# A decoder trunk on one core: one input tile taken in as two parts, three embedding products and two norms placed elsewhere

## The reference, cut to what matters

```python
def rmsnorm(x, g):  return x * lax.rsqrt(jnp.mean(x * x, -1) + EPS) * g

for i in range(DEPTH):                                   # DEPTH = 2
    f = swiglu(rmsnorm(h, P['g_f1_pre'][i]), ...)        # first feed-forward, width 2816
    h = h + 0.5 * rmsnorm(f, P['g_f1_post'][i])
    mo = mixer(rmsnorm(h, P['g_mix_pre'][i]), ...)       # pooling, short convolution, GLU convolution + layer norm
    h = h + rmsnorm(mo, P['g_mix_post'][i])
    f = swiglu(rmsnorm(h, P['g_f2_pre'][i]), ...)        # second feed-forward
    h = h + 0.5 * rmsnorm(f, P['g_f2_post'][i])
    gate = jax.nn.sigmoid(rmsnorm(h, P['g_ple_pre'][i]) @ P['w_ple_gate'][i])
    h = h + rmsnorm((p[i] @ P['w_ple_proj'][i]) * gate, P['g_ple_post'][i])
return rmsnorm(h, P['g_final'])
```

## Time and profile before

| what | value |
|---|---|
| median of three runs | 1551.94 us |
| the profiled execution's own time | 1550.16 us |
| its span, first to last instruction | 1548.2 us |
| PE busy | 1531.0 us, 99%, 10408 matmuls |
| DVE / ACT / POOL busy | 67% / 46% / 42% |
| mean granted PE clock | 0.997 |
| bytes moved | 229.31 MB, 148 GB/s on average |

### The profile page before, as it was taken

How to read it: one execution, slowest core, us unless ns; L and a number is a source line. 1 busy time by engine, 2 the same in 40 slices (tenths; PEclk the granted TensorE clock), 3 DMA queues, 4 the chain that set the end, 5 groups by cost and what they waited for, 6 DMA issues and landing times.

```text
span 1548.2 us, 28024 instructions
## 1 busy us (share of the span) xinstructions
PE 1531.0 (99%) x10408; PEld 1521.9 (98%) x10408; DVE 1034.7 (67%) x1588; ACT 713.4 (46%) x1057; POOL 643.5 (42%) x680
## 2 busy tenths in 40 slices
PE   9999999999999999999999999999999999999997
PEld 9999999999999999999999999999999999999997
DVE  7655437999876755634885553389997866555356
ACT  6333435445456433433653333355455554334346
POOL 3755203499330655500047551035973307554001
PEclk9999999999999999999999999999999999999998
DMA  6545432444443544632334454334444335445412
GB/s 221 170 154 181 172 129 84 163 151 148 163 137 109 187 161 137 226 141 93 123 125 167 144 193 169 119 110 141 159 153 148 118 128 191 157 142 213 146 70 82
DMA packets 52921, 229.31 MB, mean 148 GB/s; under 512 B 3824, under 2 KB 3952, under 8 KB 48496
## 3 DMA queue, kind: packets, MB, share of 16 engines
q1 hardware_dynamic: 52272, 226.07, 42.6%
q10 hardware_dynamic: 576, 2.26, 0.4%
HBM read 225.27 MB, written 3.04 MB: 147 GB/s over the span
## 4 chain that ended last, share of the span: by engine, by line
PE 92%; DVE 3%; issue 2%; ACT 1%; DMA 1%; POOL 0%; SPq 0%; DVEq 0%; POOLq 0%; ACTq 0%
PE ps L449 29%; PE ps L451 29%; PE ps L450 29%; PE ps L487 1%; PE ps L491 1%; PE ps L488 1%; DVE h L1184 0%; DVE w_lo_sb L1139 0%; DVE ga L1179 0%; PE ps L553 0%; DMA raw<-in_w_f_up 0%; DMA h<-in_x 0%; DVE x_lo L1194 0%; DVE ssq L1153 0%; PE ps L562 0%
## 5 line engine op out<-in xcount | busy, mean ns | idle before, releaser
L1139 DVE TENSOR_TENSOR w_lo_sb<-raw,w_hi_sb 128x1024 fp32r<-128x1024 f32 (+1 forms) x388 | 552.4, 1424 | 229.2 <-ACT w_hi_sb L812 228.5
L449 PE MATMUL ps<-x_hi,w_hi_sb 128*128 128x320 f32 x2232 | 693.1, 311 | 1.2 <-DVE w_lo_sb L1139 1.2
L451 PE MATMUL ps<-x_hi,w_lo_sb 128*128 128x320 f32 x2232 | 689.6, 309 | 0.0
L450 PE MATMUL ps<-x_lo,w_hi_sb 128*128 128x320 f32 x2232 | 689.6, 309 | 0.0
L812 ACT ACTIVATE w_hi_sb<-raw 128x1024 fp32r<-128x1024 f32 (+1 forms) x388 | 428.9, 1110 | 558.2 <-PE ps L451 465.0
L449 PEld LDWEIGHTS ps<-x_hi,w_hi_sb 128*128 128x128 f32 x2232 | 418.9, 188 | 3.2 <-DVE w_lo_sb L1139 1.1
L450 PEld LDWEIGHTS ps<-x_lo,w_hi_sb 128*128 128x128 f32 x2232 | 419.0, 188 | 0.6
L451 PEld LDWEIGHTS ps<-x_hi,w_lo_sb 128*128 128x128 f32 x2232 | 418.9, 188 | 0.0
L450 PE MATMUL ps<-mid_lo,w_hi_sb 128*128 128x320 f32 x704 | 217.4, 309 | 0.0
L449 PE MATMUL ps<-mid_hi,w_hi_sb 128*128 128x320 f32 x704 | 217.4, 309 | 0.0
L451 PE MATMUL ps<-mid_hi,w_lo_sb 128*128 128x320 f32 x704 | 217.4, 309 | 0.0
(11 more groups left out here) (209 smaller groups left out, 1636.0 us busy)
## 6 DMA issues: line engine op xcount, KB each, us to landing
raw<-in_w_f_up SPq DMA_DIRECT2D x86, 1024.0 KB, 5.3
raw<-in_w_f_dn SPq DMA_DIRECT2D x32, 1408.0 KB, 6.0
raw<-in_w_gate SPq DMA_DIRECT2D x24, 1024.0 KB, 5.3
raw<-in_w_out SPq DMA_DIRECT2D x12, 1024.0 KB, 5.2
raw<-in_w_glu SPq DMA_DIRECT2D x8, 1024.0 KB, 5.2
raw<-in_w_short SPq DMA_DIRECT2D x8, 1024.0 KB, 5.2
raw<-in_w_wo SPq DMA_DIRECT2D x8, 1024.0 KB, 5.2
raw<-in_w_pg SPq DMA_DIRECT2D x8, 1024.0 KB, 5.3
```

The costliest lines, as they stand in the source:

```text
L449: pe.matmul(out, whi, rhs_hi, start=start, stop=False, skip_group_check=True)
L450: pe.matmul(out, whi, rhs_lo, start=False, stop=False, skip_group_check=True)
L451: return pe.matmul(out, wlo, rhs_hi, start=False, stop=stop, skip_group_check=True)
L1139: dve.tensor_tensor(w_lo_sb[:, j, 0:n], raw[:, j, 0:n], w_hi_sb[:, j, 0:n].bitcast(F32), ALU.subtract).then_inc(w_lo, 1)
```

## The change

Five things change, in both layers.

At b1 the first three halves of `glu` get x tile 0 as two parts: g times the old h (tile 0), and g times f (tile 0), f being the output of the feed-forward ahead of its norm. ACT and DVE split both parts into x tiles 0 and 7 during `f1_dn`. PE multiplies the first part into the halves' own banks and the second into three others; these 18 matmuls take the place of the twelve filling ones. The chase then runs over tiles 1 to 7 and makes tile 0 last, for the fourth half alone. ACT copies the three banks of the second part to `sg`, DVE copies `bc` there, POOL multiplies the one by the other, and when DVE moves those three halves it adds the part first and then multiplies by `rb`.

At b2 three of the eight embedding products, with the part of the weights they need loaded and split during `wo`, take the place of the twelve filling matmuls. At b3 five products are left. The layer norm `ln` goes the way of `pre1`, with one wide matmul and a reciprocal of 128x320. The sums of `pre3` go from the fourth half of the first `pg` pair to the third x tile of the second pair, and their `spread` from its second to its seventh.

```diff
-        proj_raw = gate[...][:, 0:PROJ]
+        EARLY = 3
+        PROJ = (DT - EARLY) * PT * P
+        early_raw = bg[...][:, 0:EARLY_W]
-        PROJ_BANKS = (4, 5, 6, 3, 2, 0, 1, 3)
+        PROJ_BANKS = (0, 1, 2, 4, 5, 6, 3, 2)
-        SPREAD = ("post1", "ln", "post2", "post3", "pre3", "post4")
-        WIDE = (None, "pre1", "pre2")
+        SPREAD = ("post1", "post2", "post3", "pre3", "post4")
+        WIDE = (None, "pre1", "ln", "pre2")
+        def tile_at(n, i):
+            return (i + 1) % DT if n == 0 else i
+        H_PART, F_PART = 0, DT - 1
+        PART_BANKS = (2, 0, 1)
+        part_sum = [sg[:, j, :] for j in range(3)]
+        rinv_row = sg[:, 3, :]
...
# PE
+                n = new_hi[0]
+                last = DT - 2 if n == 0 else DT - 1
...
                 for k in range(DT):
                     wait_hi(k)
+                    if k > last:
+                        pe.wait_ge(x_ready, xl + k + 1)
+                        break
...
-                        sums(L, "pre3")
...
+            def h_part(L, ph, j):
+                wait_half(L, ph, 0, j)
+                pe.wait_ge(parts_lo, 2 * L + 2)
+                products(ps[:, FIRST_BANKS[j], 0:T], j, 0, x_hi[:, H_PART, :], x_lo[:, H_PART, :], True, False)
+            def f_part(L, ph, j):
+                products(ps[:, PART_BANKS[j], 0:T], j, 0, x_hi[:, F_PART, :], x_lo[:, F_PART, :], True, True).then_inc(parts_done, 1)
...
                 sums(L, "post1")
-                keep_warm(WARM_ROOT)
+                h_part(L, "glu", 0)
                 spread(L, "post1")
-                keep_warm(WARM_X, T // 2)
+                for j in (1, 2):
+                    h_part(L, "glu", j)
+                pe.wait_ge(f_out, v_f(L, 0, DT - 1))
+                for j in range(3):
+                    f_part(L, "glu", j)
                 first_pair(L, "glu", v_x(L, "b1", -1), (0, L, "b1"))
...
-                pair_of_x(L, "gate2", 0, v_moved(L, "gate2", 0), {2: sums, 3: spread}, "ln")
+                pair_of_x(L, "gate2", 0, v_moved(L, "gate2", 0), {2: wide_sums}, "ln")
...
                 sums(L, "post2")
-                keep_warm(WARM_ROOT)
+                project(L, 0)
                 spread(L, "post2")
-                keep_warm(WARM_X, T // 2)
+                for q in range(1, EARLY):
+                    project(L, q)
...
-                pair_of_x(L, "pg", 1, ..., inside={(0, 1): spread, ...})
+                pair_of_x(L, "pg", 1, ..., inside={(0, 2): sums, (0, 6): spread, ...})
...
# ACT, in chase
+                if n == 1:
+                    for q in range(1, EARLY):
+                        keep_product(L, q)
+                if n == 0:
+                    keep_part(L, 0)
...
-                    if n == 2 and m + 4 < DT:
-                        keep_product(L, m + 4)
+                    if n == 0 and m < 3:
+                        keep_part(L, m)
...
# DVE, in boundary, and where the first pair of glu is moved
                 x_low(DT - 1)
+                if n == 0:
+                    dve.tensor_copy(rinv_row, bc).then_inc(row_kept, 1)
                 split(*nxt, 3)
...
+                        if n == 0 and j < 3:
+                            dve.wait_ge(part_scaled, 3 * L + j + 1)
+                            dve.tensor_tensor(both, ps[:, FIRST_BANKS[j], 0:T], part_sum[j], ALU.add).then_inc(part_added, 1)
+                            dve.wait_ge(part_added, 3 * L + j + 1)
+                            dve.tensor_tensor(both, both, rb[:, :], ALU.mult).then_inc(moved, 1)
+                        else:
+                            move((ga, gb)[j % 2][:, j // 2, :], FIRST_BANKS[j] if n == 0 else j)
...
# POOL, at the end of boundary_x
+                if n == 0:
+                    wait_alone(row_kept, L + 1)
+                    for j in range(3):
+                        wait_alone(part_kept, 3 * L + j + 1)
+                        pool.tensor_tensor(part_sum[j], part_sum[j], rinv_row, ALU.mult).then_inc(part_scaled, 1)
```

More of the change, by code:

```diff
@@ L482, in wait_hi @@
                         pe.wait_ge(xhi_ready, v_xhi(at, b, k))
+                n = new_hi[0]
+                last = DT - 2 if n == 0 else DT - 1
                 def with_hi(j, k):
-                    w = slice(k * P, (k + 1) * P)
+                    m = tile_at(n, k)
+                    w = slice(m * P, (m + 1) * P)
                     out = ps[:, FIRST_BANKS[j], 0:T]
-                    pe.matmul(out, w_hi_sb[:, j, w], x_hi[:, k, :], start=k == 0, stop=False, skip_group_check=True)
-                    pe.matmul(out, w_lo_sb[:, j, w], x_hi[:, k, :], start=False, stop=False, skip_group_check=True)
+                    pe.matmul(out, w_hi_sb[:, j, w], x_hi[:, m, :], start=n != 0 and k == 0, stop=False, skip_group_check=True)
+                    pe.matmul(out, w_lo_sb[:, j, w], x_hi[:, m, :], start=False, stop=False, skip_group_check=True)
                 def with_lo(j, k):
-                    return pe.matmul(ps[:, FIRST_BANKS[j], 0:T], w_hi_sb[:, j, k * P:(k + 1) * P], x_lo[:, k, :],
-                                     start=False, stop=k == DT - 1, skip_group_check=True)
+                    m = tile_at(n, k)
+                    return pe.matmul(ps[:, FIRST_BANKS[j], 0:T], w_hi_sb[:, j, m * P:(m + 1) * P], x_lo[:, m, :],
+                                     start=False, stop=k == last, skip_group_check=True)
                 for j in range(3):
@@ L578, in spread, with project @@
                 mm.then_inc(bc_full, 1)
+            def project(L, q):
+                whi, wlo, at = (early_hi, early_lo, q) if q < EARLY else (proj_hi, proj_lo, q - EARLY)
+                out = ps[:, PROJ_BANKS[q], 0:T]
+                for k in range(PT):
+                    c = (at * PT + k) * P
+                    ph, pl = p_hi[:, k * T:(k + 1) * T], p_lo[:, k * T:(k + 1) * T]
+                    pe.matmul(out, whi[:, c:c + P], ph, start=k == 0, stop=False)
+                    pe.matmul(out, whi[:, c:c + P], pl, start=False, stop=False)
+                    mm = pe.matmul(out, wlo[:, c:c + P], ph, start=False, stop=k == PT - 1)
+                mm.then_inc(proj_done, 1)
             def down(L, ph, banks_left, which, n):
@@ L766, in _ @@
                 down(L, "f2_dn", v_moved(L, "f2_up", 4 * PAIRS["f2_up"] - 3), 1, 2)
[L768 to L781, removed]
                 pe.wait_ge(proj_split, L + 1)
-                for q in (0, 1):
-                    project(q)
+                for q in (EARLY, EARLY + 1):
+                    project(L, q)
                 sums(L, "post3")
-                project(2)
+                project(L, EARLY + 2)
                 spread(L, "post3")
-                for q in range(3, DT):
-                    project(q)
+                for q in range(EARLY + 3, DT):
+                    project(L, q)
                 pe.wait_ge(proj_dve, L * PROJ_DVE + PROJ_DVE)
                 first_pair(L, "pg", v_x(L, "b3", -1), (2, L, "b3"))
-                pair_of_x(L, "pg", 1, v_moved(L, "pg", 4), stat="pre3", banks_free=True, inside={(0, 1): spread, (2, 0): turn_rest_of_h} if L == LAST else {(0, 1): spread})
+                pair_of_x(L, "pg", 1, v_moved(L, "pg", 4), stat="pre3", banks_free=True, inside={(0, 2): sums, (0, 6): spread, (2, 0): turn_rest_of_h} if L == LAST else {(0, 2): sums, (0, 6): spread})
                 if L < LAST:
@@ L939, in ffn @@
                     down_step(L, dn, dn, i, i - 1, name, gain)
+                if up == "f1_up":
+                    c = COL["g_mix_pre"]
+                    act.activation(x_hi[:, H_PART, :], h[:, 0, :], ACT.Copy, scale=cur[:, c:c + 1]).then_inc(parts_hi, 1)
+                    act.wait_ge(f_out, v_f(L, 0, 0))
+                    act.activation(x_hi[:, F_PART, :], f[:, 0, :], ACT.Copy, scale=cur[:, c:c + 1]).then_inc(parts_hi, 1)
                 down_step(L, dn, after, 0, PAIRS[dn] - 1, name, gain, last=True)
@@ L1076, in _ @@
                     for j in range(4):
+                        if (pair, j) == (0, 1):
+                            act.wait_ge(early_proj_in, L * 16 + 16)
+                            act.activation(early_hi, early_raw, ACT.Copy).then_inc(early_proj_hi, 1)
                         act.wait_ge(halves_done, v_half(L, "wo", pair, j) + 4)
@@ L1188, in x_low @@
                 def x_low(m):
+                    t = tile_at(n, m)
                     if m == 0:
@@ L1289, in ffn @@
                     down_step(L, dn, i, i - 1, name)
+                if up == "f1_up":
+                    c = COL["g_mix_pre"]
+                    for n, (src, t) in enumerate(((h, H_PART), (f, F_PART))):
+                        dve.wait_ge(parts_hi, 2 * L + n + 1)
+                        dve.scalar_tensor_tensor(x_lo[:, t, :], src[:, 0, :], cur[:, c:c + 1],
+                                                 x_hi[:, t, :].bitcast(F32), ALU.mult, ALU.subtract).then_inc(parts_lo, 1)
                 down_step(L, after, 0, PAIRS[dn] - 1, name, last=True)
```

124 lines of the change are left out of this document (82 added, 42 removed).

## The result

The changed kernel takes 1563.97 us (median of 4 runs, 1563.42 to 1565.88), the kernel before 1551.56 in the same session: a ratio of 1.008, 95% interval 1.0067 to 1.0093, so 12.4 us slower. I had forecast 1554.6 and a range up to 1558.5. The profiled span went from 1548.2 to 1561.8.

A forecast was written before the change was run, and what follows sets the result against it. PE was taken to bound the kernel, with 92% of the chain of waits. 2 x (0.5 + 0.35 - 0.6) + 1.6 + 0.6 = +2.7 gave 1552.9 profiled, 1554.6 us as a median; range 1551.0 to 1558.5.

The forecast's parts named there:

- b1: Start of glu: later splits and added DVE work cost +0.5 us per layer, bounds -0.2 and +1.5.
- the fourth half's wait: In glu: PE waits about 1.5 us for DVE's w_lo; the half begins some 0.25 us later than before.
- The short wait: Ahead of the fourth half of glu's second pair: 0 to 0.7 us, taken as 0.25, with 1.6 of room.
- Rival B: At b1, POOL's multiplies hold DVE: 1.5 us more per layer, +5.7 in all, 1557.6 us; chance 0.18.
- b2: Embedding product 0 ahead of spread makes spread later: +0.35 us per layer, bounds 0 and +0.55.
- `ln`: Layer norm: one wide sum replaces sums and spread, -0.6 us (0.57) per layer, bounds -0.6 and +0.5.
- `pg` in layer 0: PE waits ahead of the second pair, first move later: +1.6 us, bounds +0.9 and +2.0; PE then idles 2.7.
- In layer 1: End of pg: chain let be 1.0 us later, ACT's last sigmoid late; +0.6 us, bounds +0.2 and +1.6.
- Rival C: Layer 0, sums of post4: PE's clock falls after idling, some 20 matmuls cost +3 us, 1557.6 us; chance 0.09.
- Rival A: In glu and pg: splits keep up, every removed matmul is gained, -8.4 us, 1543.5 us; chance 0.08.

The follow-up runs named there:

- e9: Kernel before with one more DVE instruction per layer, the split of the fourth half of glu's second pair made twice; 1554.73 us against 1551.21 (1.0020).
- e5: Changed kernel without POOL's three multiplies, the second parts added unscaled; 1557.66 us (1.0038), 6.3 less than the changed kernel.
- e6: Changed kernel without DVE's three adds of the second parts, which POOL still scales; 1560.47 us (1.0051), 3.5 less than the changed kernel.
- e8: Changed kernel with 20 more filling matmuls ahead of the sums of post4 in layer 0; 1563.22 us (1.0069).
- e2: Changed kernel with the sums and spread of pre3 back at their old places in pg; 1560.25 us (1.0056), 3.7 less than the changed kernel.
- e7: Changed kernel with DVE's copy of bc behind the split of glu's fourth half instead of ahead of it; 1562.34 us (1.0065).
- e10: Kernel with b1 and pg taken back, product 0 at b2 halved around spread, twelve filling matmuls ahead of layer 0's pre3 sums; 1551.15 us (0.9998).
- both taken back: Changed kernel with its b1 and pg parts both taken back, leaving ln, b2 and b3 changed; 1550.62 us (0.9996).
- e4: Kernel before with nothing but the wide sum for ln; 1550.73 us (0.9995).

## Why the prediction was wrong, by its steps

- **b1 failed, in where it closed DVE's account.** "The room is just used up: 0 to 0.7 of wait, and I take 0.25", and with it +0.5 per layer with +1.5 as the upper bound. The direction was right and the fourth half's wait came (1.10 idle where I said about 1.5), but from b1 to the mean of `ln` the change cost 3.0 and 6.2. The short wait that I had set ahead of the second pair's fourth half did not come; PE waited 1.25 ahead of that pair's first half and then in `out0`. I closed the account at the last instruction I had worked out, the split of the second pair's fourth half, as if DVE caught up behind it. It does not: e9 shows 1.2 us that this room covers and that is lost later all the same. The profile before had held a warning. Behind the x_lo at 253.91 the timeline marks only 0.29 us of idle time for DVE until 372.70, in `out0`, so the question was not how much room one half has but where DVE is next idle:

```profile
269.52 0.49 DVE L1253 TENSOR_TENSOR ga<-ps,rb 128x320 f32<-128x320 f32 x1 [0.29 <-POOL cbuf L1672]
...
372.70 1.23 DVE L1139 TENSOR_TENSOR w_lo_sb<-raw,w_hi_sb 128x1024 fp32r<-128x1024 f32 x1 [0.81 <-ACT w_hi_sb L812]
```

Two smaller slips are in the same step. With my own terms at their high end (2.15 + 0.5 against 1.6 + 0.25) the wait was 0.8, not 0.7. And my upper bounds add up to +8.7, or 1560.6, while the range stopped at 1558.5; the measured 1563.97 lies above both.

- **Rival B was part of what happened at b1**: it had 0.18, and with POOL's multiplies left out 1.7 and 2.1 us of the loss stay. I gave the multiplies 0 to 0.5 in the sum, from one overlap that had cost 0.17. That overlap was no price for a whole multiply: DVE's add began at 248.69, when only 0.30 of POOL's operation was left (it ended at 248.99). The three multiplies cost 0.50 on a copy and 0.97 on three squares (e5), and 1.3 and 4.1 us of the two layers' time, where B had 1.5 for each. In layer 0 the parts nearly make up the whole: 1.3 for the multiplies (e5) and 1.3 for the adds (e6) of 3.0; 0.4 is left, about the size of DVE's copy of `bc` (0.48), which no run left out. The Trainium skill ("SBUF — State Buffer", section "SBUF: two separate sides") calls the port pair of GpSimd and VectorE an exclusive lock, by which a DVE operation on two SBUF operands stands still; here the trace agrees, with 2.66 against 1.69 for three adds of squares, which read two tiles in SBUF, with and without the multiplies. The copy, which reads one, was held too, 1.00 against 0.50.
- **b2 and `ln` were right**: +0.37 (forecast +0.35) and -0.46 (forecast -0.57, summed as -0.6) per layer.
- **`pg` in layer 0 was right in each step**: PE waits ahead of the second pair, the first move 1.6 later, PE idle 2.78 ahead of the sums of `post4` (forecast 2.7). In layer 1 the end is 1.1 later, inside my bounds, against +0.6; the spread of `pre3` came 1.55 later there, where I let the chain be 1.0 later without a row for it.
- **Rival C came with it**, at half my price or less: 1.4 in this trace and 0.75 to 1.35 in four others instead of 3, shown by e8; no row stood behind the 20 matmuls in that price. It came once more in `out0` of layer 1, where 2.6 of the 4.2 lost are wait and the rest is the low clock. No kernel kept PE busy there, but the clock fell there in all five traces that keep b1 with POOL's multiplies (the changed kernel, e2, e6, e7, e8) and in none of the others. I had given it 0.09 while my own forecast contained the idle PE of 2.7 us that it starts from.
- Rival A did not come, and of the missing matmuls little: with the statistics early again PE mostly waits at them, and 0.4 to 0.5 of 2.65 us is gained per layer (e2).

Not settled: why layer 1's `out0` waits 2.4 us where layer 0's waits 0.8. There DVE's split at 1138.66 waited for ACT, ACT for POOL, and POOL's multiplies took up to twice their time, so that the three seem to have delayed each other; nothing was run that separates them.

## What to carry to other kernels

An instruction added to an engine is not paid where it stands but where that engine is next waited for. Follow its row of instructions until it is really idle, and close the sum there; room ahead of one consumer is no cover if the engine is full behind it. When work on PE is cut in a stage whose pace another engine sets, look at how long PE then idles: the low clock afterwards can be a second cost. Twenty filling matmuls kept it away in e8; in e10 twelve kept it away where they stood, and it fell some 20 us later.

## What the runs showed of the hardware that was not expected

The length of PE's idle time alone does not tell whether the clock falls. Ahead of the sums of `pre3` it was idle 1.51 us with `pg` taken back and 1.50 with both taken back; the clock stayed at 1.00 in the one and fell to a mean of 0.66 in the other. Behind `pg` the mended kernel has the same short waits as the kernel before (0.57 and 0.40 us against 0.58 and 0.40), and the windows differ. First the kernel before, then the mended one:

```profile
770.00:775.00 5.00, 3.63 (x26) 3.24 (x25) 4.89 (x11) 1.80 (x4) 0.00 (x0) 1.00 0.63 210
```

```profile
770.00:775.00 5.00, 5.00 (x23) 4.76 (x22) 4.83 (x12) 1.86 (x4) 0.00 (x0) 0.53 0.63 210
```

Twelve filling matmuls and three products less ran at b3 ahead of them, but that does not decide it. The kernel of e4 is the kernel before from b2 on, has the same waits behind `pg` (0.58 and 0.40), and its clock fell:

```profile
770.00:775.00 5.00, 4.91 (x27) 4.62 (x26) 4.89 (x10) 1.75 (x4) 0.00 (x0) 0.70 0.64 210
```

So the same stretch of program can run at either level, and one trace does not show that an edit made the clock fall or kept it. The kernel before differs in this from execution to execution as well: its mean clock lies between 0.994 and 0.997. In e4 the fall cost 0.05 us up to the next wide sum.

And DVE and POOL delayed each other both ways: POOL's three multiplies took 3.59 us beside DVE, 1.20 each, where an operation of that size took 0.90.
